# Three tiles together in the differential mixer, one sigmoid table in the recurrent mixer, and new places and orders for chunks and tiles in the hybrid layers

## The reference

```python
h = rms_norm_2(x, ln_mix_pre[l])
x = x + rms_norm_2(hybrid_mixer(h, ...), ln_mix_post[l])
h = rms_norm_2(x, ln_ffn_pre[l])
x = x + rms_norm_2(conv_ffn(h, ...), ln_ffn_post[l])
```

## Time and profile before

| | |
|---|---|
| time, median of 3 runs | 2613.99 us (2608.9 to 2615.21) |
| the profiled execution | 2613.67 us, span 2611.8 us |
| PE, PEld busy | 96%, 86% of the span |
| DVE, ACT, POOL busy | 73%, 56%, 7% |
| instructions | 38904 |
| granted TensorE clock, mean | 0.983 |

### The profile page before, as it was taken

The page is one execution under the profiler, slowest core; times in us unless marked ns, Lnnn a source line. Parts: engine busy times, 40 slices in busy tenths (PEclk is TensorE's granted clock), DMA queues, the critical chain, the costliest instruction groups (busy, mean ns, idle before and its releaser), DMA issues.

```text
span 2611.8 us, 38904 instructions
## 1 busy us (share of the span) xinstructions
PE 2516.3 (96%) x15915; PEld 2244.3 (86%) x15915; DVE 1918.9 (73%) x2417; ACT 1471.7 (56%) x1808; POOL 180.0 (7%) x187
## 2 busy tenths in 40 slices
PE   7998999999999999999999999999999999999999
PEld 7766889999889888888888888888798999888998
DVE  7886366544666598989898988888865786676873
ACT  2213355444564477777777777777735564435653
POOL 0100012212010000000000000000000121000220
PEclk9998999999999899999999999999999999999999
DMA  7231054554424299999999999999952465362550
GB/s 236 90 107 44 1 162 147 179 191 151 146 82 135 80 385 373 356 349 361 371 361 344 372 355 366 350 370 366 340 166 81 130 209 178 97 194 66 190 182 33
DMA packets 339048, 567.60 MB, mean 217 GB/s; under 512 B 17576, under 2 KB 184724, under 8 KB 338740
## 3 DMA queue, kind: packets, MB, share of 16 engines
q1 hardware_dynamic: 325942, 556.29, 61.4%
q10 hardware_dynamic: 12926, 8.77, 1.2%
HBM read 563.97 MB, written 2.24 MB: 217 GB/s over the span
## 4 chain that ended last, share of the span: by engine, by line
PE 84%; DVE 9%; ACT 4%; issue 2%; SPq 0%; DMA 0%; DVEq 0%; ACTq 0%; POOL 0%; POOLq 0%
PE bank L210 23%; PE bank L212 22%; PE bank L211 22%; PE bank L2136 3%; DVE chunks_lo L334 2%; ACT chunks_hi L325 2%; PE bank L3349 1%; PE bank L1771 1%; PE bank L1754 1%; PE bank L3299 1%; PE bank L677 1%; PE bank L2695 1%; PE bank L2682 1%; PE bank L2696 1%; PE bank L697 1%
## 5 line engine op out<-in xcount | busy, mean ns | idle before, releaser
L3467 DVE TENSOR_TENSOR weight_lo<-ring,weight_hi 128x2048 fp32r<-128x2048 f32 x336 | 766.5, 2289 | 111.8 <-ACT weight_hi L3325 110.4
L3325 ACT ACTIVATE weight_hi<-ring 128x2048 fp32r<-128x2048 f32 x336 | 643.5, 1918 | 206.9 <-PE bank L212 206.2
L334 DVE TENSOR_TENSOR chunks_lo<-ring,chunks_hi 128x2048 fp32r<-128x2048 f32 x171 | 395.1, 2310 | 293.2 <-ACT chunks_hi L325 292.8
L325 ACT ACTIVATE chunks_hi<-ring 128x2048 fp32r<-128x2048 f32 x171 | 325.9, 1906 | 242.1 <-PE bank L212 241.0
L210 PE MATMUL bank<-x_parts,chunks_hi 128*128 128x256 f32 x1408 | 404.6, 287 | 12.9 <-DVE x_parts L414 7.7
L211 PE MATMUL bank<-x_parts,chunks_hi 128*128 128x256 f32 x1408 | 399.0, 283 | 0.0
L212 PE MATMUL bank<-x_parts,chunks_lo 128*128 128x256 f32 x1408 | 399.0, 283 | 0.0
L210 PE MATMUL bank<-weight_hi,xg_hi 128*128 128x512 f32 x896 | 352.7, 394 | 0.8 <-DVE xg_lo L3473 0.8
L212 PE MATMUL bank<-weight_hi,xg_lo 128*128 128x512 f32 x896 | 349.3, 390 | 0.0
L211 PE MATMUL bank<-weight_lo,xg_hi 128*128 128x512 f32 x896 | 348.9, 389 | 0.0
L210 PEld LDWEIGHTS bank<-x_parts,chunks_hi 128*128 128x128 f32 x1408 | 270.7, 192 | 16.6 <-DVE x_parts L414 4.7
(11 more groups left out here) (545 smaller groups left out, 4812.9 us busy)
## 6 DMA issues: line engine op xcount, KB each, us to landing
ring<-in_moe_w_gate SPq DMA_DIRECT2D x112, 1024.0 KB, 6.7
ring<-in_moe_w_up SPq DMA_DIRECT2D x112, 1024.0 KB, 6.7
ring<-in_moe_w_down SPq DMA_DIRECT2D x112, 1024.0 KB, 6.9
ring<-in_w_up SPq DMA_DIRECT2D x44, 1024.0 KB, 5.1
ring<-in_w_in SPq DMA_DIRECT2D x24, 1024.0 KB, 5.6
ring<-in_w_down SPq DMA_DIRECT2D x22, 1024.0 KB, 4.9
ring<-in_xa_w_kv SPq DMA_DIRECT2D x16, 1024.0 KB, 5.8
ring<-in_da_w_qkv SPq DMA_DIRECT2D x12, 1024.0 KB, 5.1
```

Of the source, the lines that this page charges most:

```text
L325: act.activation(self.home(n)[0], ring[:, c.slot], ACT.Copy)\
L334: dve.tensor_tensor(lo, ring[:, c.slot], hi.bitcast(F32), ALU.subtract)\
L3325: act.activation(weight_hi[:, slot(m, odd + next_)], ring[:, m % ROUND], ACT.Copy).then_inc(weights_hi.sem, 1)
L3467: dve.tensor_tensor(weight_lo[:, at_], ring[:, m % ROUND], weight_hi[:, at_].bitcast(F32), ALU.subtract)\
```

## The change

In the recurrent mixer the sigmoid table is loaded ahead of the last but one r tile, and the four gate multiplications are interleaved with the two bonus multiplications. In the differential mixer the first three tiles go together. In the hybrid layers `fv` 0 gets the spare bank 4, `fk` 2 stands ahead of the three `dec` products (the chunk that its column frees is still turned to after the last `dec`), and `add_y` adds the first part of h at once. Ahead of the feed-forward part chunk `left` is rounded behind the third pair of the output projection, in a place of its own; `left + 1` gets other places; from `left + 2` on the three places are shifted by one (`turned`, `behind`), so that `left + 2` is rounded in `add_and_begin` and one chunk further is begun in `conv_ffn`, its rest now behind the remade x. The scratch places of the first x and of `xf` move.

```diff
@@ Weights
             def home(self, n):
-                return self.homes.get(n) or (self.hi[:, n % SPLITS], self.lo[:, n % SPLITS])
+                s_ = (n + sum(n >= a for a in self.turned)) % SPLITS
+                return self.homes.get(n) or (self.hi[:, s_], self.lo[:, s_])
@@ upper
-                if n >= SPLITS and n not in self.homes:
-                    act.wait_ge(tiles_done.sem, self.done[n - SPLITS])
+                old = self.behind.get(n, n - SPLITS)
+                if old >= 0 and n not in self.homes:
+                    act.wait_ge(tiles_done.sem, self.done[old])
@@ rows3
-        def rows3(pe, c, t, x, ready=None):
-            b = next_bank(pe)
+        def rows3(pe, c, t, x, ready=None, spare=None):
+            if spare is None:
+                b = next_bank(pe)
+            else:
+                b = spare
+                tile_no[0] += 1
@@ diff_mixer
-                for n in range(N):
-                    if n < 2 * DT:
-                        marks.append(tile3(pe, chunk_of(n), n % 2 * P, x_parts, ready if n == 0 else None))
+                marks.extend(together3(pe, [(chunk_of(n), n % 2 * P) for n in range(3)], x_parts, ready))
+                for n in range(2, N):
+                    if 2 < n < 2 * DT:
+                        marks.append(tile3(pe, chunk_of(n), n % 2 * P, x_parts))
+                    elif n > 2:
+                        marks.append(rows3(pe, chunk_of(n), n % 2, x_parts))
                     else:
-                        marks.append(rows3(pe, chunk_of(n), n % 2, x_parts))
-                    if n == 1:
                         sum_x(pe, rows=True)
@@ out_to_banks
-            down_sums(made, y, lambda act, b: weights.upper(act, c0 + b + SPLITS),
-                      lambda dve, b: weights.lower(dve, c0 + b + SPLITS), False)
+            def upper(act, b):
+                weights.upper(act, c0 + b + SPLITS)
+                if b == 2:
+                    weights.upper(act, c0 + 3 + SPLITS)
...
+            down_sums(made, y, upper, lower, False)
@@ add_y
-                    if 1 <= n <= DT:
-                        dve.wait_ge(scaled.sem, scaled.at(n))
-                        dve.tensor_tensor(h[:, n - 1], h[:, n - 1], y[:, n - 1], ALU.add)\
-                           .then_inc(added.sem, added.tick())
-                    if n >= 2:
+                    m = 0 if n == 0 else n - 1
+                    if n != 1 and m < DT:
+                        dve.wait_ge(scaled.sem, scaled.at(m + 1))
+                        dve.tensor_tensor(h[:, m], h[:, m], y[:, m], ALU.add).then_inc(added.sem, added.tick())
+                    if n == 1:
+                        after(dve, 0)
+                    if n > 2:
                         after(dve, n - 2)
@@ add_and_begin
-                weights.lower(dve, left)
                 weights.lower(dve, left + 1)
+                weights.lower(dve, left + 2)
...
-                    if n == 5:
-                        weights.upper(act, left)
                 weights.upper(act, left + 1)
+                weights.upper(act, left + 2)
@@ hybrid
-                     ("sw", 2), ("fk", 0), ("fk", 1), ("dec", 0), ("dec", 1), ("dec", 2), ("fk", 2)]
+                     ("sw", 2), ("fk", 0), ("fk", 1), ("fk", 2), ("dec", 0), ("dec", 1), ("dec", 2)]
...
-            used_up = {key: c for c, key in last_of.items()}
+            used_up = {("dec", 2) if key == ("fk", 2) else key: c for c, key in last_of.items()}
...
-                return bank[(first + place[key]) % 4]
+                return bank[4 if key == ("fv", 0) else (first + place[key]) % 4]
@@ conv_ffn
-            release(DT * T)
+            release(5 * CHUNK)
...
-                return c0 + n // 2 + SPLITS + 1 if n % 2 and 3 <= n < NT - 1 else None
+                return c0 + n // 2 + SPLITS + 1 if n % 2 and 5 <= n < NT - 1 else None
...
-                weights.upper(act, c0 + SPLITS + 1)
+                weights.upper(act, c0 + SPLITS + 2)
...
+                    if n == 4:
+                        act.wait_ge(tiles_done.sem, marks[BEGUN - 1])
...
-                weights.lower(dve, c0 + SPLITS + 1)
                 for n in range(NT + 1):
...
                                 rest_of_x(dve, k - 2)
+                        weights.lower(dve, c0 + SPLITS + 2)
@@ front, scalar engine
+                        if f == NF - 2:
+                            act.preload_act_table_set(SIGMOID)
@@ rwkv, vector engine
+                dve.wait_ge(glu_made.sem, glu_made.at(4))
                 for u_ in range(2):
+                    for j in (2 * u_, 2 * u_ + 1):
+                        dve.wait_ge(gated.sem, gated.at(j + 1))
+                        dve.tensor_tensor(gu[:, j], gu[:, j], sg[:, j], ALU.mult)
                     dve.wait_ge(summed_up.sem, summed_up.at(u_ + 1))
...
-                for j in range(4):
-                    dve.wait_ge(gated.sem, gated.at(j + 1))
-                    dve.tensor_tensor(gu[:, j], gu[:, j], sg[:, j], ALU.mult)
@@ the loop over the layers
-            x_first = parts_at(4 * CHUNK - 1024, f"x_first{l}", 2, DT, T)
+            x_first = parts_at(3 * CHUNK, f"x_first{l}", 2, DT, T)
             left = p_["o"] + 3 + SPLITS
-            weights.homes[left + 1] = (parts_at(OP_AT, f"third_hi{l}", CHUNK)[:, :], parts_at(2 * CHUNK - 512, f"third_lo{l}", CHUNK)[:, :])
+            places = [parts_at(a, f"home{l}{n}", CHUNK)[:, :] for n, a in enumerate((CHUNK, 2 * CHUNK, OP_AT, 0))]
+            weights.homes.update({left: (places[0], places[1]), left + 1: (places[2], places[3])})
+            weights.turned.append(left + 2)
+            weights.behind.update({left + 2: left - SPLITS, left + 3: left - 2, left + 4: left - 1})
```

More of the change, by code:

```diff
@@ L33 @@
 LN_EXP = "natural_log_exp_and_others"
+SIGMOID = "sigmoid_and_others"
 def const_arrays():
@@ L301, in __init__ @@
                 self.lo = parts_at(W_AT + SPLITS * CHUNK, "chunks_lo", SPLITS, CHUNK)
-                self.chunks, self.done, self.homes = [], [], {}
+                self.chunks, self.done, self.homes, self.behind, self.turned = [], [], {}, {}, []
                 self.rounded, self.rest = sig("weights_hi"), sig("weights_lo")
@@ L1335, in _, with lower @@
                         weights.done[c] = tiles_done.total
-            down_sums(made, y, lambda act, b: weights.upper(act, c0 + b + SPLITS),
-                      lambda dve, b: weights.lower(dve, c0 + b + SPLITS), False)
+            def upper(act, b):
+                weights.upper(act, c0 + b + SPLITS)
+                if b == 2:
+                    weights.upper(act, c0 + 3 + SPLITS)
+            def lower(dve, b):
+                weights.lower(dve, c0 + b + SPLITS)
+                if b == 2:
+                    weights.lower(dve, c0 + 3 + SPLITS)
+            down_sums(made, y, upper, lower, False)
         def down_sums(made, y, upper=None, lower=None, load=True):
@@ L1543, in _ @@
                     if kind in ("fv", "av"):
-                        marks[key] = rows3(pe, *column[key], x_parts)
+                        marks[key] = rows3(pe, *column[key], x_parts, None, bank[4] if key == ("fv", 0) else None)
                         if key == ("fv", 1):
```

## The result

The changed kernel takes 2593.86 us (median of 4 runs, 2591.8 to 2595.73) against 2614.6 of the kernel before (4 runs, 2608.9 to 2617.11): ratio 0.9926, 95% interval 0.9913 to 0.9939. Measured once more beside the last experiments it was 0.9934 (0.9921 to 0.9948). By these ratios 17.2 and 19.3 us are won (by the medians 17.9 and 20.7) where 14.45 were forecast. The two profiled executions stand at 2613.67 and 2593.96, 19.7 apart; their spans 2611.8 and 2592.2.

A forecast was written before the change was run, and what follows sets the result against it. The prediction took the kernel to be bound by matmuls, PE holding 84% of the chain. Its terms summed to 14.45 us, from 2613.67 to 2599.2 us, with a range of 2595 to 2606.5.

The forecast's parts named there:

- points 1 and 2: Recurrent mixer: earlier sigmoid table load, 0.95 us won, and gate multiplications interleaved with the bonuses, 0.9 us won.
- points 4 and 5: Both hybrid layers: `fv` 0 in the spare bank, 1.7 us each, and `fk` 2 ahead of `dec`, 1.6 us each.
- 1, the table: Recurrent mixer's fence: with the sigmoid table loaded earlier, PE starts at its transposes' end; 0.95 us, bounds 0 and 1.28.
- The estimate of 2597.8 for a longer load: Sigmoid table: if a load took about 2.7 us, it would hide 1.4 us more, giving some 2597.8.
- 2, the gates: End of the recurrent mixer's bonus products: two gate multiplications move into DVE's wait; 0.9 us, bounds 0 and 1.4.
- 3, three tiles: Differential mixer's start: three tiles together let `sum_x` start earlier; 2.6 us, bounds 1.3 and 2.9.
- point 4: Both hybrid layers: `fv` 0 in the spare bank moves PE's 1.72 us pause; 1.7 us each, bounds 0.2 and 2.2.
- 6 and 7, the feed-forward part: `add_y` gives 0.4 us between layers, 0.1 worse in `finish`; chunks ahead of the convolutions with `add_y` give 2.0 and 1.1.
- My chain for the thirteenth tile: First convolution: its chunk's lowering ends at 2086.1, PE alone there at 2086.0, today's start 2088.15; 2.0 us with `add_y`.
- the clock follows the moved pauses: Rival: the clock falls behind both new hybrid-layer pauses, 0.2 us won at each, time 2602.2; chance 0.12.
- conversions hold the path: Rival: ACT and DVE bring evictions one chunk late in hybrid and convolution parts; 10.5 us won, time 2603.1; chance 0.14.
- the loops take it back: Rival: starts move but the loops behind take it back; some 7 us won or less, 2607 and above; chance 0.10.

The follow-up runs named there:

- the filled kernel: Kernel before plus four idle TensorE products behind the last bonus product, in the 3.63 us pause ahead of the recurrent mixer's second phase; ratio 0.9986.
- the later product: Changed kernel with the differential mixer's small product behind the fourth tile and ScalarE's exponential of it behind the third square; ratio to the kernel before 0.9935.
- the hybrid orders alone: Kernel before with only the spare bank for `fv` 0 and `fk` 2 ahead of the `dec` products, in both hybrid layers; ratio 0.9985.

## Why the prediction was right, point by point

The mechanism came as forecast and the sum was too small: 14.45 us against 17.2 and 19.3. The mis-sized term is the clock at the pauses of the recurrent mixer, which the sum put at nothing (points 1 and 2). My bounds shared that fault, and they were added up wrongly: all lower ones together give 4.1 (I wrote 6), all upper ones 18.4 (I wrote 19), so the first measurement lies above every upper bound together. In part two errors offset each other by luck: points 4 and 5 were too large by the time of their own experiment.

Fourteen profiles stand at hand, and each edit is in six or seven of them. That gives a mean of each stretch with and without its edit, over whatever the clock did:

| records | edit | without: mean (range) | with: mean (range) | less | forecast |
|---|---|---|---|---|---|
| 700 to 880 | table | 44.09 (42.24 to 46.91) | 41.20 (41.19 to 41.21) | 2.89 | 0.95 |
| 880 to 900 | gates | 5.68 (5.38 to 5.80) | 4.57 (4.44 to 4.87) | 1.11 | 0.9 |
| 900 to 1900 | (gates, behind) | 122.45 (122.09 to 122.72) | 120.95 (120.55 to 122.83) | 1.50 | 0 |
| 1900 to 4050 | none | 268.23 | 267.87 | 0.36 | 0 |
| 4050 to 6100 | three tiles | 304.26 (303.59 to 304.59) | 301.72 (300.20 to 303.86) | 2.53 | 2.6 |
| 10600 to 11050 | bank, `fk` 2 | 64.38 (63.41 to 64.75) | 61.38 (61.18 to 61.61) | 2.99 | 3.3 |
| 11400 to 12200 | chunks, `add_y` | 108.20 (107.27 to 108.80) | 105.28 (104.46 to 106.20) | 2.92 | 2.0 |
| 13200 to 13650 | bank, `fk` 2, `add_y` | 69.91 (69.38 to 70.32) | 67.26 (66.08 to 68.25) | 2.65 | 3.7 |
| 13650 to 14800 | chunks, `add_y` | 157.96 | 156.60 (156.10 to 156.98) | 1.35 | 1.1 |
| 14800 to the last record | `add_y` in `finish` | 140.36 | 140.49 | -0.13 | -0.1 |

(In the third row the filled kernel is left out of "without". In the fourth, which no edit touches, the profiles are parted by the gates. In the row of the second layer, "with" means bank and `fk` 2.) The sum is 18.2 against 14.45.

**1, the table.** The path term holds: 1.04 us at full clock (42.24 to 41.20). What failed is its size: I costed the pause of 0.95 by its length alone. Without the edit the clock fell in six of seven profiles between records 700 and 880, for 1.6 to 4.7 us; with it in none of seven. In four of the six the fall came 2 us behind the pause; in two it came only some 25 us later, at 210.1, at a pause of 0.47 that all kernels have, and why the edit ends that one is open. The upper bound of 1.28 knew only the load. A fall costs 1.6 here (43.88 against 42.24), more than the 1.3 that I counted for one. The estimate of 2597.8 for a longer load has no support: the load that moved takes 1.28 too.

**2, the gates.** 0.94 at full clock (5.38 to 4.44), as forecast. The mis-sized term is again the clock, 1.5 us in the phase behind; the filled kernel has the same gain without the path.

**3, three tiles.** 2.5 against 2.6, and the pause ahead of the small product costs nothing, as the later product shows. One sentence was wrong: "fed three tiles, PE should not fall". It fell behind the new pause of 1.34 in four of the five profiles that have it, hidden by the same loop.

**4 and 5, hybrid layers.** In the profiles the pauses did what I said, and the slack of 0.4 ahead of `aq` was enough. None of ten moved pauses (two layers, five profiles) was followed by the lower level, where the old pauses of 1.72 were in ten of sixteen. As a saving of time the two points were too large, 3.9 for 6.6 alone. In the second layer of the changed kernel the clock fell within the pause of 3.14 ahead of the layer's first part of x, at 2231.5. The same fall is in the traces of three kernels with the old order (70.2 to 70.3 us), where the one behind the old pause is then missing; so it takes back a part of point 4 when it comes: 68.25 us against 66.45 without it.

**6 and 7, the feed-forward part.** The first x comes 0.32 earlier (3.15 for 3.47), not 0.4, and `finish` is 0.13 worse. The first convolution wins 2.9 where I counted 2.0. My chain for the thirteenth tile ended on DVE at 2086.1; in fact PE hardly stands (0.16 us in sum), and the tile starts at 36.2, which is PE's own time without the lower level that the first tiles had in the kernel before (13.07 us for the first 96 matmuls, 12.47 now). Two profiles of variants have that stretch at the lower level as the kernel before has it, and there the tile starts at 36.8: the path is 1.9 shorter, and with the first x 2.2, where I counted 2.0. The rest is the clock. The second layer gives 1.35 against 1.1, and its wait of 1.10 stayed.

**Rivals.** That the clock follows the moved pauses: not in the hybrid layers, though it did in the differential mixer, where it cost nothing. That conversions hold the path: no trace shows it, but the time of the hybrid orders alone doesn't speak against something of its size. That the loops take it back: no. The clock did decide the size, but by pauses that went, in a place where I had priced only the path.

**Open.** The sum of the separate ratios, 0.19 + 0.12 + 0.15 + 0.20 = 0.66%, agrees with the whole, but each has an uncertainty of 0.1. Where the hybrid orders' missing 2.7 us go isn't shown by a trace. Why the second phase was slow (122.8) in one of six profiles behind the pause of 2.69, and in all six behind 3.63, is not settled. Nearly half of the 1.9 us, 0.8 to 0.9, lies between records 1700 and 1900, some 86 us behind that pause: 36.2 us in the six with 3.63 and in the slow profile, 35.2 to 35.5 in the others. The row of 0.36 us without an edit is open too; more than half of it is one profile that lacks a fall of the clock there.

## What to carry to other kernels

A pause of TensorE has two prices: its length on the path, and the lower clock behind it, which idle products in the pause could save here even where the path stays. Price a moved wait by what stands next behind it in the ring of banks; a pause ahead of a loop that other engines bound cost nothing (1.34 us here). Compare stretches between landmarks over several profiles, and whole executions at the same granted clock, before a difference of 2 us is put down to an edit. A lower level that an edit removes in one place may come in another: count it as won only if the mean clock rises.

## What the runs showed of the hardware that was not expected

- Identical instructions on the same stretch (records 700 to 880, no edit in it) took 42.24 to 46.91 us in seven profiles, by the clock alone; from record 4500 to 6100 the same instructions took 239.82 to 243.43 in three profiles.
- A pause as short as 0.95 us in otherwise busy work was followed, in six of seven profiles, by a fall of the clock up to record 880 (in four of them 2 us behind it); without the pause in none of seven. A pause of 1.72 us was followed by one in ten of sixteen cases.
- Four idle products more made the kernel faster, 0.9986 (0.9977 to 0.9995), and its mean clock rose from 0.983 to 0.985.
